# Loads of w_in in rows of 4 KB: pairs of column blocks, half of the rows each

## The reference, cut to what matters

```
h = RMSNorm(x)
u, q, k, v, f, g = split(h @ w_in)          # 512 x4, 8, 2 x 1024 columns; w_in is 1024 x 4104
pool_out = PoolMixer(u)                     # window means of 2, 4, 8, 16 tokens, then 4 small matrices
att      = attention(q, k, v, log_sigmoid(f))   # prompt: causal; samples: 1024 cached tokens of each, in pages
y  = sigmoid(g[0]) * (pool_out @ w_up_pool) + sigmoid(g[1]) * (att @ w_up_att)
x += y @ w_out
x += HierMoE(RMSNorm(x))                    # 1 of 4 groups, 2 of its 8 experts; expert: silu(x w1) * (x w3) @ w2
return RMSNorm(x), and the new k, v, log f and pooling rows
```

## Time and profile before

| | us |
|---|---|
| median of 3 runs | 774.1 |
| the profiled execution | 774.42 |
| its span | 772.5 |
| PE busy | 614.4 (80%) |
| DVE busy | 233.0 (30%) |
| ACT busy | 85.8 (11%) |
| POOL busy | 52.7 (7%) |
| bytes moved, mean rate | 269.14 MB, 348 GB/s |

### The profile page before, as it was taken

The page is one execution under the profiler, slowest core; times in us unless marked ns, Lnnn a source line. Parts: engine busy times, 40 slices in busy tenths (PEclk is TensorE's granted clock), DMA queues, the critical chain, the costliest instruction groups (busy, mean ns, idle before and its releaser), DMA issues.

```text
span 772.5 us, 13852 instructions
## 1 busy us (share of the span) xinstructions
PE 614.4 (80%) x6169; PEld 375.2 (49%) x6169; DVE 233.0 (30%) x603; ACT 85.8 (11%) x231; POOL 52.7 (7%) x66
## 2 busy tenths in 40 slices
PE   3999987898879997799858777785777677677864
PEld 3787754666657353455434343443444344334432
DVE  3007475889733145222211111111111111111113
ACT  2023221112210111000000000000000000000003
POOL 0503381121000000000000000000000000000000
PEclk8899988999999997799988897798789888977998
DMA  9997458999997823699999999999999999999992
GB/s 217 284 382 262 151 171 294 373 353 310 377 348 293 338 108 139 241 415 425 420 415 424 422 418 420 424 420 419 421 421 419 421 423 418 422 420 419 421 376 94
DMA packets 45051, 269.14 MB, mean 348 GB/s; under 512 B 5076, under 2 KB 5896, under 8 KB 34487
## 3 DMA queue, kind: packets, MB, share of 16 engines
q1 hardware_dynamic: 38672, 228.81, 75.5%
q0 software_dynamic: 3712, 37.28, 12.4%
q10 hardware_dynamic: 2607, 2.14, 0.9%
HBM read 265.99 MB, written 2.46 MB: 348 GB/s over the span
## 4 chain that ended last, share of the span: by engine, by line
DMA 40%; PE 39%; SPq 9%; DVE 7%; issue 3%; ACT 1%; DVEq 0%; ACTq 0%
DMA ring<-w_up 36%; PE bank L1301 9%; PE bank L1377 8%; SPq L466 8%; PE bank L1469 5%; DMA ring<-w_in 4%; PE bank L1530 4%; PE bank L1515 3%; DVE ring L984 1%; PE bank L1284 1%; PE bank L1317 1%; SPq L532 1%; PE bank L1446 1%; DVE front L988 1%; PE bank L1332 1%
## 5 line engine op out<-in xcount | busy, mean ns | idle before, releaser
L1301 PE MATMUL bank<-ring,front 128*32 128x256 f32 x2048 | 167.9, 499 | 101.8 <-DMA ring<-w_up 97.8
L1301 PEld LDWEIGHTS bank<-ring,front 128*32 128x32 f32 x2048 | 91.9, 141 | 170.0 <-issue 146.6
L1172 DVE COPY front<-bank 128x256 f32<-128x256 f32 x32 | 13.6, 424 | 243.8 <-PE bank L1301 243.8
L1377 PE MATMUL bank<-hT,ring 128*128 128x264 f32 x256 | 60.6, 400 | 6.5 <-DMA ring<-w_in 6.5
L1469 PE MATMUL bank<-hT,ring 128*128 128x264 f32 x256 | 62.7, 399 | 2.3 <-DMA ring<-w_in 2.3
L1317 PE MATMUL bank<-ring,front 128*32 128x256 f32 x1024 | 62.2, 384 | 0.7 <-DVE front L1177 0.7
L1377 PEld LDWEIGHTS bank<-hT,ring 128*128 128x128 f32 x256 | 50.3, 197 | 16.0 <-issue 6.9
L1469 PEld LDWEIGHTS bank<-hT,ring 128*128 128x128 f32 x256 | 48.8, 196 | 18.7 <-issue 7.8
L1284 PE MATMUL bank<-front 128*32 128x256 f32 (+1 forms) x768 | 54.9, 401 | 0.8 <-DVE front L1088 0.8
L800 ACT ACTIVATE front<-bank 128x128 f32<-128x128 f32 x32 | 8.9, 278 | 388.3 <-PE bank L1309 388.3
L1317 PEld LDWEIGHTS bank<-ring,front 128*32 128x32 f32 x1024 | 33.6, 112 | 23.7 <-issue 1.6
(11 more groups left out here) (290 smaller groups left out, 504.8 us busy)
## 6 DMA issues: line engine op xcount, KB each, us to landing
ring<-w_up SPq DMA_DIRECT2D x31, 2048.0 KB, 30.9
ring<-w_down SPq DMA_DIRECT2D x31, 2048.0 KB, 34.6
ring<-w_gate SPq DMA_DIRECT2D x31, 2048.0 KB, 34.3
ring<-w_in SPq DMA_DIRECT2D x8, 2048.0 KB, 19.9
ring<-w_out SPq DMA_DIRECT2D x2, 2048.0 KB, 11.8
front<-q_scratch POOLq DMA_DIRECT2D x8, 256.0 KB, 8.2
ring<-w_up_pool SPq DMA_DIRECT2D x1, 2048.0 KB
ring<-w_up_att SPq DMA_DIRECT2D x1, 2048.0 KB, 19.8
```

What stands on the lines that cost most here:

```text
L1301: last = m.matmul(bank[GATEUP][32 * g:32 * g + 32, 0:256], xgT[:, k % 2, k // 2], w[:, k, 256 * (g % 2):256 * (g % 2) + 256], start=k == 0 ...
L1377: last = m.matmul(out[:, 0:TOK], w[:, k, n * P:(n + 1) * P], hT[:, k, 0:TOK], start=k == 0, stop=k == DK - 1)
```

## The change

Two neighbouring blocks of 512 columns are loaded together, 1024 columns or 4 KB of a row, in two loads of half of the k rows each (k = 0 to 3, and 4 to 7). Item ("w", 0) and ("w", 1) are now the halves of the columns of u and q, ("w", 2) and ("w", 3) those of k and v; ("g", 0) and ("g", 1) are gates 0 to 7, ("g", 2) and ("g", 3) gates 8 to 15. Each load still moves 2 MB. A `proj` or `gate` step waits for both loads of its pair and takes k rows 0 to 3 from one slot and 4 to 7 from the other. First and last steps in `uses` change accordingly, and with them the slots. The arithmetic and PLAN stay as they are.

```diff
--- before.py
+++ after.py
@@ -305,8 +305,10 @@
         PLAN += [("merge", n) for n in range(DK)] + [("out", 0), ("norm", 0), ("route", 0)]
 
 
-        uses = {("w", c): (("proj", c), ("proj", c)) for c in range(4)}
-        uses.update({("g", n): (("gate", GPS * n), ("gate", GPS * n + GPS - 1)) for n in range(4)})
+        order = [a for step, a in PLAN if step == "proj"]
+        halves = {i: [a for a in order if a // 2 == i // 2] for i in range(4)}
+        uses = {("w", i): (("proj", halves[i][0]), ("proj", halves[i][1])) for i in range(4)}
+        uses.update({("g", n): (("gate", DK * (n // 2)), ("gate", DK * (n // 2) + DK - 1)) for n in range(4)})
         for b in range(NS):
             uses["K", b] = ("keys0", b), ("keys3", b)
             uses["V", b] = ("dpv", b), ("dpv", b)
@@ -445,8 +447,8 @@
             return taken[b], n + 1
 
 
-        last_use = {("w", c): ("proj", c, CC - 1) for c in range(4)}
-        last_use.update({("g", n): ("gate", GPS * n + GPS - 1) for n in range(4)})
+        last_use = {("w", i): ("proj", halves[i][1], CC - 1) for i in range(4)}
+        last_use.update({("g", n): ("gate", DK * (n // 2) + DK - 1) for n in range(4)})
         last_use.update({("V", b): ("dpv", b) for b in range(NS)})
         last_use.update({("up", 0): ("up", DK - 1), ("up", 1): ("merge", DK - 1), ("out", 0): ("out", 2 * PB - 1), ("out", 1): ("out", 2 * PB - 1)})
 
@@ -495,10 +497,10 @@
                     sp.wait_ge(*count_used(last))
                 dst, done = slot[where[item]], s_slot[where[item]]
                 if kind in "wg":
-                    first = a * DC if kind == "w" else W_GATE + a * DC
-                    sp.dma_start(dst.rearrange("p (k n) -> p k n", k=DK),
-                                 w_in[:, first:first + DC].rearrange("(p k) n -> p k n", p=P)).then_inc(done, 16)
-                    if item == ("w", C_K):
+                    first, ks = a // 2 * D + (W_GATE if kind == "g" else 0), slice(DK // 2 * (a % 2), DK // 2 * (a % 2) + DK // 2)
+                    sp.dma_start(dst.rearrange("p (k n) -> p k n", k=DK // 2),
+                                 w_in[:, first:first + D].rearrange("(p k) n -> p k n", p=P)[:, ks]).then_inc(done, 16)
+                    if item == ("w", 3):
                         sp.wait_ge(s_pad, 4)
                         sp.dma_start(wf[:, :, 0:HEADS], w_in[:, W_FORGET:W_FORGET + HEADS].rearrange("(p k) n -> p k n", p=P)).then_inc(in_wf, 16)
                 else:
@@ -571,7 +573,7 @@
                 ins = g.memset(tile[:, :, 0:PAD], 0.0)
             ins.then_inc(s_zero, 1)
             pool.wait_ge(s_ridx, 1)
-            pool.wait_ge(s_slot[where["w", C_K]], 16)
+            pool.wait_ge(s_slot[where["w", 1]], 16)
             for b in range(NS):
                 g.indirect_dma_start(lfT[:, b].rearrange("p i h -> p (i h)"), None, t["cache_logf"][0].rearrange("g (q r) h -> (g q) (r h)", r=RLEN),
                                      bass.IndirectOffsetOnAxis(ridx[:, b:b + 1], 0), bounds_check=NPHYS * RUNS - 1).then_inc(in_lfp, 16)
@@ -1368,13 +1370,14 @@
 
             for step, a in PLAN:
                 if step == "proj":
-                    w = wait_loaded(pe, "w", a).rearrange("p (k n) -> p k n", k=DK)
+                    w = [wait_loaded(pe, "w", 2 * (a // 2) + i).rearrange("p (k n) -> p k n", k=DK // 2) for i in range(2)]
                     for n in range(CC):
                         out = free("proj", a, n)
+                        cols = slice(a % 2 * DC + n * P, a % 2 * DC + (n + 1) * P)
                         for k in range(DK):
                             if a == C_Q and n == 0:
                                 pe.wait_ge(s_hT, max(k, 1) + 2)
-                            last = m.matmul(out[:, 0:TOK], w[:, k, n * P:(n + 1) * P], hT[:, k, 0:TOK], start=k == 0, stop=k == DK - 1)
+                            last = m.matmul(out[:, 0:TOK], w[k // 4][:, k % 4, cols], hT[:, k, 0:TOK], start=k == 0, stop=k == DK - 1)
                         last.then_inc(filled[turn["proj", a, n][0]], 1)
                 elif step == "nat":
                     g = 32 * ((C_Q, C_K, C_V, C_U).index(a))
@@ -1462,11 +1465,11 @@
                     pe.wait_ge(s_spool, 1)
                     m.matmul(out[:, 0:TOK], wpool[:, a], pooledT[:, a], start=True, stop=True).then_inc(filled[turn["mix", a][0]], 1)
                 elif step == "gate":
-                    w = wait_loaded(pe, "g", a // GPS).rearrange("p (k n) -> p k n", k=DK)
+                    w = [wait_loaded(pe, "g", 2 * (a // DK) + i).rearrange("p (k n) -> p k n", k=DK // 2) for i in range(2)]
                     out = free("gate", a)
-                    cols = slice((a % GPS) * P, (a % GPS + 1) * P)
+                    cols = slice((a % DK) * P, (a % DK + 1) * P)
                     for k in range(DK):
-                        last = m.matmul(out[:, 0:TOK], w[:, k, cols], hT[:, k, 0:TOK], start=k == 0, stop=k == DK - 1)
+                        last = m.matmul(out[:, 0:TOK], w[k // 4][:, k % 4, cols], hT[:, k, 0:TOK], start=k == 0, stop=k == DK - 1)
                     last.then_inc(filled[turn["gate", a][0]], 1)
                 elif step == "scores":
                     outs = [free("scores", a, f) for f in range(2)]
```

## The result

The changed kernel takes 790.4 us (median of 4 runs, 788.88 to 793.08), the kernel before on the same chip 773.9: a ratio of 1.0208, 95% interval 1.0172 to 1.0245, so 16.5 us slower. The forecast was 786.8, the range 775 to 801. The profiled execution is the slowest of the four, 793.1 us with a span of 791.2, which is 18.7 above the span before. "Gate 8" is the 16 matmuls of the step (`gate`, 8), and so on.

The account below looks back on a forecast made before the run. PE's path before expert 3's first load at 312 us was taken as the bound, the DMA-full expert phase moving as a block. 2.5 - 3.5 + 13.2 + 2.8 - 2.3 = +12.7 on 774.4 gave 787.1, median-adjusted 786.8; range 775 to 801.

Parts of the forecast that it names:

- The start: q's first products, at 18.70 us before, wait for 4.2 MB instead of 2.1 MB: +2.5 us.
- The fast end of 0.6: Low end for q's first products: remaining bytes come at 393 GB/s, products start at 19.2 us, +0.6.
- 90 to 128 us: V0 lands late, but DVE's wait for row 2's queries goes and V1 limits next: -3.5 us, ends -7 and +1.
- Gate 8: g3 can't be issued before gate 7 ends, then shares bandwidth with V4 and K6: +13.2 us, low end 5.3.
- The high end given for this term, 18: At gate 8: g2 and g3 at 243 GB/s, or g3 served only with the last of both page loads.
- the 175 to 182 given as a sign: Predicted time in us at which the chain's w_in piece ends at gate 8, PE at half clock behind it.
- The clock behind it: PE runs at half clock after the wait at gate 8, 1.8 us in that step and 1.0 next: +2.8.
- 196 us: PE's wait for w_in before gate 12 goes, since gates 8 to 15 come together: -2.3 us.
- The expert phase as a block: From expert 3's first load to the end, the length stays as now, within 2 us; only its start moves.
- Rival A: Row length doesn't matter, w_in keeps its mixed speeds; start +6.1, gate 8 +18: +21.1, 795 us; chance 0.22.
- Rival B: At gate 8, g3 lands 11.9 us after issue, the page loads' median: +2.9, 777 us; chance 0.15.
- C: 103 to 127 us decides: queries and V1 early, -7; g3 lands within 9 us: -3.4, 770.7 us; chance 0.08.

Follow-up runs that it names:

- e6: Kernel before, with SP holding the second gate load (g1) back until the queries of row 2 have landed: ratio 0.9952, 771.6 us.
- e2: Kernel before, with only the gates loaded in pairs and u, q, k, v as single loads: ratio 1.0144, 787.1 us.
- e3: Changed kernel, with POOL's gather of V4, and K6 and the queries behind it, held until g3 has landed: ratio 1.0063, 781.4 us.
- e4: Changed kernel, same slots and waits, each 2 MB load issued as two 1 MB transfers with 2 KB rows: ratio 1.0300, 798.2 us.
- e5: Kernel before, with the columns of w1 and w2 exchanged, and those of g1 and g2; only its times mean something: 769.8 us, one run.
- e10: Kernel before, k loaded and projected first, gate blocks ordered 0, 2, 1, 3, second gate load held until row 2's queries landed: ratio 0.9972, 773.8 us.
- e8: Kernel before, with g1 held until row 2's queries landed and k loaded and projected ahead of q: ratio 0.9934, 771.6 us.
- e1: Kernel before, with only u, q, k and v loaded in pairs and the gates as before: ratio 1.0011, 776.3 us.
- e7: Kernel before, with k loaded and projected ahead of q: ratio 0.997, 773.5 us.
- e9: Kernel before, with k loaded and projected ahead of q and the gate blocks in the order 0, 2, 1, 3: ratio 0.9922, 769.0 us.

## Why the prediction came out right

The direction, the place and the mechanism held; the sum of 12.7 us was 4.4 short of the 17.1 measured ahead of expert 3, and 1.6 more lie in the expert phase of that one execution. That 786.8 came so near the median of 790.4 is in part luck: the start was costed 2.1 us too high, which hides a part of the 5.2 by which gate 8 was costed too low. The terms, in the order of the prediction:

- **The start: +2.5 forecast, +0.4 measured** (19.10 against 18.70), and even that is no more than the start differs between kernels with the same first loads (18.70, 18.82 in e6, 19.26 in e2). The fast end of 0.6 was the answer, since 4 KB rows ran at 377 GB/s in 8 to 16 us. Mixing in the measured 6.1 us was wrong: those were w2 behind a w1 that had taken all the time until 18.6 at the slow speed, and the paired w0 and w1 had no slow part.
- **90 to 128 us: -3.5 forecast, -3.2 measured.** Gate 4 starts 2.84 earlier (133.15 against 135.99), with the 0.4 of the start still in it. V0 landed 11.9 us after its issue and PE waited 3.5, V1 landed after about 10 and PE waited 2.4, the query wait went. What I did not foresee is gate 6 at a lower clock, +1.7, so that gate 7 is only 1.15 early. The granted clock was 0.66 in 150 to 155; ahead of it PE had idled 2.06 us, as the kernel before does at the same place at full clock. In e2 and e3 gate 6 took 5.49 us as well, in e4 3.80, so why it fell stays open.
- **Gate 8: +13.2 forecast, +18.4 measured** from gate 7's start to gate 8's (25.45 against 7.02). This is the mis-sized term. The step that failed is "with its 40.6% share of the queues' packet time and 1.63 MB in 10 us, 163 to 170 GB/s, g3's 2.1 MB take 12.3 us". With V4 and K6 both queued, SP's queue had 28.0% and 114 GB/s in 172 to 183 us. The share of the earlier trace rows wasn't a constant of the queues. The high end given for this term, 18, was the measured one, for the second of its two reasons: V4 and K6, issued at 162.64 and 164.00, were both in by 181.8, and g3 only at 183.4, while w_in itself wasn't slow. That the end lies at 183.5, outside the 175 to 182 given as a sign, is the same miss. e3 confirms the rest: without the gathers 8.8 remain.
- **The clock behind it: +2.8 forecast, +2.4 measured** (6.15 against 3.73 us at gate 8).
- **196 us: -2.3 forecast, -2.4 measured** (the lag falls from 19.7 behind gate 8 to 17.25 at gate 12). No V was waited for in the later rows. What follows up to expert 3 changes the lag by 0.1.
- **The expert phase as a block:** 461.7 against 460.1 us, within the 2 us named.

Rival A is refuted by the 377 and 406 GB/s, and e4 puts a size on it: 7.8 us with 2 KB rows, where A and the forecast were 8 apart. A's condition "w_in keeps its mixture of speeds" was the wrong alternative, though. e5 showed that the mixture is by place in the row, so that pairing a slow with a fast block had to change it in any case. Rival B needed g3 in 11.9 us and C in 9; e3 shows that it takes 12.1 even when the pages stay away. The Trainium skill, "DMA: Bandwidth & Descriptors", Specifications, gives 512 B as the least transfer for line rate. That agrees with half of the blocks (393 GB/s), not with those at 160 to 210 GB/s in 2 KB rows and with a full DMA share. The same page of the Trainium skill, Queues, rings and completion order, tells of turns between queues packet by packet, where a packet can hold several descriptors; whether the packets that the profile counts are those, no run shows. In 172 to 183 us the profile counts 322 packets of SP and 281 of POOL, near equal numbers, but POOL's were larger (10.8 against 3.9 KB on the mean), so g3 got well under half of the bytes, where the prediction read equal turns as half. In the earlier trace rows it was 404 to 184, though, so equal numbers aren't the rule either, and what sets the shares stays open.

## What to carry to other kernels

Before pairing or merging loads, write down for each the earliest issue (the last use of what had its slot) and its first use; if there is only one step between the two, the load's whole time is on the path, however fast it is. Then look at what the same event releases on other queues: two page gathers brought the landing time of a 2 MB load from 12.1 to 21.5 us, and the held load of e10 fell into the same trap (18.1 us); in e6 and e8 the held load was late too, but there it was a slow block. A faster transfer pays only where somebody waits for it: the start gained nothing from twice the rate in e1, and 4 us in e7 from loading the fast block first, of which 2.3 were left at the end.

## What the runs showed of the hardware

- **The speed of a strided load depends on the place of its columns.** Rows of 2 KB out of a matrix with a row pitch of 16416 B: blocks 1 and 3 came at 160 to 210 GB/s, blocks 0 and 2 at 310 to 430, both with a DMA share of 0.9 or more, and e5 moved the slow speed with the columns. The pitch shifts each row by 32 B against a multiple of 4096, so over 128 rows blocks of either kind begin at the same set of places within 4096 B; where a single row begins doesn't explain it. Rows of 4 KB came at 372 to 406. Both kinds in transfers issued one behind the other (e4) came at 339 on the mean of 8 to 26 us, more than the 234 that equal bytes at 167 and at 393 would give (an estimate). What does this wasn't tried and stays open.
- **A small copy suffers from a bulk load on another queue whatever its speed.** The 256 KB broadcast of the queries landed after 3.6 us alone, 4.4 with g1 held back (e6), 10.3 behind a slow block, and 8.7 behind a fast one (e9).
- **Shares between queues aren't constant.** Beside page gathers SP's weight load had 28.0% of the packet time and 114 GB/s in the changed kernel, 40.6% and 163 in the earlier trace rows, 52.6% and 168 in e10. In e8, with the slow block in 118 to 128 us, it had 99.1% and 190, and POOL's queue moved 0.16 MB, although a gather had been issued at 119.8. What they depend on wasn't tried.
